# Attention block: merge of the two branches bank by bank, a gate input projected earlier, a key tile split earlier

## The chip, the cores and the metric

The kernel runs on one core of a Trainium2 chip. The metric is the device time in microseconds of one execution. Of the kernel before, three timed runs are given: 1705.27, 1705.39 and 1705.43 us, median 1705.39 us.

## The reference

Two transformer blocks over 256 tokens of width 1024 in float32. The change touches only the attention part of the second block:

```python
h = rms_norm_2(x, attn_norm_g)
q, k, v, f_logit, cb, cc, cu, ga, gb = split(h @ w_in)      # widths 512 x3, 8, 512 x3, 1024 x2
q, k = rms_norm_2(q per head, q_norm_g), rms_norm_2(k per head, k_norm_g)      # 8 heads of 64
log_f = log_sigmoid(f_logit + b_f)
y_att = forgetting_attention(q, k, v, log_f)      # causal softmax, logits plus the cumulated log_f
y_conv = cb * causal_short_conv(cc * cu, conv_w)
merged = sigmoid(ga) * (y_att @ w_out_att) + sigmoid(gb) * (y_conv @ w_out_conv)
x = x + merged @ w_o
```

Before it lie the first block (a mixer and a dense network, a mixer and eight experts), behind it a router with 16 experts in four groups and a last gated projection.

## The kernel before, in words

**Weights.** All weights come as tiles of 128 x 2048 float32 (1 MB). The SP queue loads them in one fixed order into a ring of six slots. Each tile is split in two float32r parts, so that a product is three matmuls (`three`, L1080: high x high, high x low, low x high): ACT copies the tile to `w_high` (`high(T)`, L671), then DVE makes `w_low` as the difference (`low(T)`, L1597). There are three places for split tiles, so `high(T)` waits until PE has used tile T-3. A slot of the ring is free, and SP loads tile T+6 into it, when `low(T)` is done. Every engine has its work in an order written out by hand; waits are semaphores (`used(eng, name)`: PE has used the tile).

**The tiles of this block**, counted from B: q 0, 1; k 2, 3; v 4, 5; cb 6, 7; cc 8, 9; cu 10, 11; four gate inputs of two tiles each 12 to 19; out_conv2 20, 21; out_att 22, 23; o 24 to 27. Tiles 28 and on belong to the expert stage behind.

**PE.** The eight PSUM banks hold 512 columns each. `project_T` (L1087) makes half of an input transposed in one bank, with 48 matmuls of 256 columns per tile. The order is: the eight columns of the forget gates, q (banks 0, 1), a small transpose for the gate logits, k (2, 3), v (4, 5), the cumulated gates in bank 7, mean squares of q in banks 6 and 7, the first cb tile, mean squares of k in banks 6 and 7, the second cb tile (4, 5), then cc (0, 1) after `qk_hat` 1 and cu (2, 3) after `qk_hat` 2 (L1470). Then eight gate tiles alternate in banks 4 and 5, with the attention's logits, transposes and value products between them. `out_chunks` (L1539) projects the two branches transposed, out_conv2 into banks 4 to 7 and out_att into banks 0 to 3, each with two tiles of 48 matmuls; a bank holds two of the eight chunks of model columns. Last `rows_of_model` (L1114) multiplies the merged rows with o, 24 matmuls of 512 columns per tile, into banks 4 to 7. In front of it stand six filler matmuls, `spare(4, 6)` (L1563).

**DVE and ACT at the start.** `move_logits` (L1842) copies the forget gates' sums out, does `low(B+2)` and waits for the transpose on PE. Then DVE and ACT hand the log-sigmoid to and fro (`log_step`), and only behind it stand `high(B+3)` (L923) on ACT and `low(B+3)` on DVE.

**q-hat and k-hat.** ACT takes the square root of the mean squares (`qk_std`), DVE a reciprocal of 1024 columns and a product (`qk_hat`): q-hat goes to `h`, which frees banks 0 and 1; k-hat goes to `uT`, which frees 2 and 3. `low(B+9)` stands between the two, `low(B+10)` behind the second.

**The merge.** DVE multiplies the sigmoid of gb with banks 4 to 7 (`conv_gated`). When half of out_att is whole (`rows_half`, two banks) `merge(0)` (L2184) multiplies the sigmoid of ga, 1024 columns, with two banks and adds the other branch; `merge(1)` does the rest; ACT copies each half to `hT_high` (L1003), and `merged_low` (L2189) makes the difference in `hT_low`. `low(B+25)` stands in front of `merge(0)`. PE waits for half m // 2 in front of tile m of o (L1565).

Of the kernel before, what the change touches and what calls it, by code (L numbers as in the profile page):

```python
# [16 lines left out]
KC = D // P  # L17
# [84 lines left out]
def build(nc, A, out):  # L102
    ctx = ExitStack()
    with ctx:
# [110 lines left out]
        def bank(b, n=1):  # L215
            return PS[:, b:b + n, :].rearrange("p b n -> p (b n)")
# [64 lines left out]
        ple_moved, logits_moved = sem("ple_moved"), sem("logits_moved")  # L281
        HALF_MIX, HALF_FFN, HALF_ATT, HALF_O, HALF_PLE, HALF_PG = (1, 5), 3, 7, 8, 10, 11
        BY_TILE = (1, 2, 3, 6)
# [20 lines left out]
        stored = sem("stored")  # L304


        def slot(s):
# [133 lines left out]
        def sparse_segment(e, s):  # L441
            assert s.base == len(names)
            stream.segment(e.made(s), e.trips)
            for i in range(e.trips):
# [11 lines left out]
        w2 = A["w_in_2"][0]  # L456
        two = [("q", 0), ("k", 512), ("v", 1024), ("cb", 1544), ("cc", 2056), ("cu", 2568),
               ("ga0", 3080), ("ga1", 3592), ("gb0", 4104), ("gb1", 4616)]
# [15 lines left out]
        def used(eng, name):  # L474

            eng.wait_ge(split_used, split_at[name] + 1)
# [170 lines left out]
        def _(act):  # L647
# [23 lines left out]
            def high(T):  # L671

                name = names[T]
                w = stream.arrived(act, name, 0 if name[0] in ("moe", "moe2") else None)
                if T >= SPLITS:
                    act.wait_ge(split_used, T - SPLITS + 1)
                act.activation(w_high[:, T % SPLITS, :], slot(w), ACT.Copy).then_inc(split_high, 1)  # L677
# [237 lines left out]
            B = BASE[4]  # L915
            high(B + 2)


# [3 lines left out]
            act.activation(hs[:, 4:6, :], hs[:, 2:4, :], ACT.Ln, bias=ones[:, 0:1]).then_inc(log_step, 1)  # L922
            high(B + 3)  # L923
            used(act, ("q", 1))
# [16 lines left out]
            act.activation(wk[0][:], bank(4, 2), ACT.Copy).then_inc(cbu_copied, 1)  # L941
            for T in range(10, 14):
                high(B + T)
            used(act, ("cu", 1))
            act.activation(wk[1][:], bank(2, 2), ACT.Copy).then_inc(cbu_copied, 1)
            high(B + 14)

# [54 lines left out]
            high(B + 25)  # L1002
            for k in range(2):  # L1003
                act.wait_ge(mT_sum, k + 1)
                act.activation(hT_high[:, 4 * k:4 * k + 4, :].rearrange("p c s -> p (c s)"), sgu[:, k, :],
                               ACT.Copy).then_inc(mT_high, 1)
# [22 lines left out]
        def _(pe):  # L1029
# [5 lines left out]
            def spare(b, n, part=router2_pair):  # L1035

                for k in range(n):
                    mm(PS[:, b, 0:320], flat_cols(part)[:, 0:P], flat_cols(part), start=True, stop=True)
# [430 lines left out]
            project_T(("cb", 1), 5)  # L1469
            for name, b, value in (("cc", 0, 1), ("cu", 2, 2)):  # L1470
                pe.wait_ge(qk_hat, value)
                for hf in range(2):
                    project_T((name, hf), b + hf)

# [44 lines left out]

            pe.wait_ge(qk_std, 2)  # L1520
            pe.wait_ge(cbu_copied, 1)
            gate(0, lambda step: logits(0, step // 2) if step % 2 else None)
            pe.wait_ge(cbu_copied, 2)
            pe.wait_ge(cc_used, 1)
# [14 lines left out]
            def out_chunks(name, b, half):  # L1539

                for m in range(2):
                    T = have((name, m))
                    wh, wl = split(w_high, T, 2), split(w_low, T, 2)
                    for c in range(KC):
                        a = slice(c * P, (c + 1) * P)
                        for k in range(2):
                            f = half + 2 * m + k
                            last = three(chunks(b, 4)[:, c, :], (wh[:, k, a], wl[:, k, a]),
                                         (yT_high[:, f, :], yT_low[:, f, :]),
                                         m == 0 and k == 0 and c % 2 == 0, m == 1 and k == 1, True)  # L1550
                        if name == "out_att" and m == 1 and c == 3:
                            last.then_inc(rows_half, 1)
                    last.then_inc(split_used, 1)

            pe.wait_ge(yconv_low, 1)
            pe.wait_ge(gates_act, 8)
            pe.wait_ge(att_yT, 1)
            out_chunks("out_conv2", 4, 4)
            pe.wait_ge(att_yT, 2)
            out_chunks("out_att", 0, 0)  # L1560
            pe.wait_ge(mT_sum, 1)
            pe.wait_ge(conv_gated, 2)
            spare(4, 6)  # L1563
            for m in range(4):
                pe.wait_ge(merged, 1 + m // 2)  # L1565
                rows_of_model(("o", m), h_rows, 4, m == 0, m == 3)
# [10 lines left out]
        def _(v):  # L1577
# [15 lines left out]
            def rest_of(out_, whole, part):  # L1593

                return tt(out_, whole, part.bitcast(F32), ALU.subtract)  # L1595
# [246 lines left out]
            def move_logits(b, n, k, between=None):  # L1842

                v.wait_ge(logits_ready, 2 * k - 1)
                copy(small_sums[0:2 * n, :], PS[0:2 * n, b, 0:S]).then_inc(logits_moved, 1)
                if between:
                    between()
                v.wait_ge(logits_ready, 2 * k)
# [217 lines left out]

            move_logits(6, HEADS, 2, lambda: low(B + 2))
            sums = PS[:, 7, 0:4 * HEADS].rearrange("p (t a e) -> p t a e", t=TT, a=2)
# [9 lines left out]
            stt(out=lf[:], in0=lf[:], scalar=0.0, in1=hs[:, 4:6, :], op0=ALU.min, op1=ALU.subtract).then_inc(log_step, 1)  # L2078
            for T in range(3, 8):
                low(B + T)  # L2080
# [8 lines left out]
            for o in range(2):  # L2089
# [3 lines left out]
            last.then_inc(qk_hat, 1)  # L2093
            low(B + 9)
            v.wait_ge(qk_std, 2)
            own.link(nc.vector.reciprocal(wk[3], wk[3]))
            stt(out=uT[:], in0=chunks(2), scalar=pcol[:, 37:38], in1=r[1], op0=ALU.mult,
                op1=ALU.mult).then_inc(qk_hat, 1)
            for T in range(10, 14):
                low(B + T)  # L2100

            v.wait_ge(cbu_copied, 2)
            cu = wk[1].rearrange("p (c s) -> p c s", c=CH)
# [77 lines left out]
            low(B + 24)  # L2181
            low(B + 25)

            def merge(k):  # L2184

                own.link(tt(sgu[:, k, :], sgu[:, k, :], bank(2 * k, 2), ALU.mult))
                tt(sgu[:, k, :], sgu[:, k, :], sgu[:, 2 + k, :], ALU.add).then_inc(mT_sum, 1)

            def merged_low(k):  # L2189

                v.wait_ge(mT_high, k + 1)
                rest_of(hT_low[:, 4 * k:4 * k + 4, :].rearrange("p c s -> p (c s)"), sgu[:, k, :],
                        hT_high[:, 4 * k:4 * k + 4, :].rearrange("p c s -> p (c s)")).then_inc(merged, 1)

            v.wait_ge(conv_gated, 2)
            v.wait_ge(rows_half, HALF_ATT)
            merge(0)
            used(v, ("out_att", 1))
            merge(1)
            merged_low(0)  # L2200
            merged_low(1)
            for T in range(26, 30):
                low(B + T)
# [31 lines left out]
```

## Time and profile before

| what | us |
|---|---|
| median of three timed runs | 1705.39 |
| the profiled execution | 1702.37 |
| its span, first to last instruction | 1700.6 |
| PE busy | 1629.0 |
| DVE busy | 1287.8 |
| ACT busy | 1015.0 |

The span and what lies around it (1.8 us) make the profiled execution's time. Times in the trace count from the first instruction. A matmul's record is longer than the distance at which the next one can start. Idle time is told with the instruction that ended it, under what released that; on an engine that is not late it costs nothing. The attention block lies between about 1262 and 1466 us.

### The profile page before, as it was taken

The page shows a single profiled execution, that of the slowest core. Times are in us where ns is not written, and L with a number is a line of the kernel's source. Part 1 is how long each engine was busy: PE and PEld are TensorE (multiplying, and loading weights), DVE is VectorE, ACT ScalarE, POOL GpSimd, SP SyncE. Part 2 cuts the span into 40 slices and gives each one's busy share as a digit, 9 for nine tenths or more (in the row PEclk, how much of TensorE's full clock was granted, in tenths as well). Part 3 has the DMA queues.
Part 4 walks back from the last instruction along what each step waited for, and adds up shares of the span by engine and source line. Part 5 has one row for each costly group of instructions (what it writes and reads, how often), then busy time and mean ns, then how long its engine had stood idle before and what let it go on. Part 6 is the DMA issues. An engine that isn't in the chain of part 4 may idle for free.

```text
span 1700.6 us, 23910 instructions
## 1 busy us (share of the span) xinstructions
PE 1629.0 (96%) x9497; PEld 1335.6 (79%) x9497; DVE 1287.8 (76%) x1147; ACT 1015.0 (60%) x882; POOL 21.7 (1%) x41
## 2 busy tenths in 40 slices
PE   6999999998899999999999999999979999899997
PEld 6979999897677776777767677777768898788886
DVE  5984444698688889888898888888855665568875
ACT  4654343466576767777676777766624453367753
POOL 2000000000000000000000000000000000000000
PEclk9999999999999999999999999999989999999999
DMA  9536656433598989999898998989854434469970
GB/s 285 199 112 199 197 175 197 136 125 119 207 372 311 369 304 369 344 343 377 307 373 301 373 369 316 374 307 385 297 186 149 149 124 149 136 213 309 306 260 26
DMA packets 240906, 431.54 MB, mean 254 GB/s; under 512 B 11556, under 2 KB 121664, under 8 KB 240832
## 3 DMA queue, kind: packets, MB, share of 16 engines
q1 hardware_dynamic: 239344, 426.17, 71.4%
q10 hardware_dynamic: 1488, 4.34, 0.7%
q8 instruction: 51, 0.84, 0.2%
q14 instruction: 23, 0.19, 0.0%
HBM read 429.44 MB, written 1.05 MB: 253 GB/s over the span
## 4 chain that ended last, share of the span: by engine, by line
PE 74%; issue 13%; DVE 9%; ACT 3%; DMA 1%; POOL 0%; DVEq 0%; ACTq 0%; SPq 0%; POOLq 0%
PE PS L1083 22%; PE PS L1085 22%; PE PS L1084 22%; DVE w_low L1595 3%; PE PS L1171 2%; PE PS L1300 2%; DVE x_res L1948 1%; PE PS L1353 1%; ACT w_high L677 1%; DVE h L1612 1%; ACT w_high L830 1%; DVE hT_low L1595 1%; DMA ring<-in_w_in_dram 1%; PE PS L1480 0%; ACT L830 0%
## 5 line engine op out<-in xcount | busy, mean ns | idle before, releaser
L1595 DVE TENSOR_TENSOR w_low<-ring,w_high 128x2048 fp32r<-128x2048 f32 x402 | 918.0, 2289 | 281.9 <-ACT w_high L677 147.6
L830 ACT ACTIVATE w_high<-ring 128x2048 fp32r<-128x2048 f32 x306 | 586.0, 1918 | 244.4 <-PE PS L1085 244.2
L1083 PE MATMUL PS<-w_high,hT_high 128*96 128x512 f32 (+3 forms) x1184 | 416.6, 352 | 9.9 <-DVE hT_low L1595 5.7
L1085 PE MATMUL PS<-w_high,hT_low 128*96 128x512 f32 (+3 forms) x1184 | 413.5, 349 | 0.0
L1084 PE MATMUL PS<-w_low,hT_high 128*96 128x512 f32 (+3 forms) x1184 | 411.9, 348 | 0.0
L677 ACT ACTIVATE w_high<-ring 128x2048 fp32r<-128x2048 f32 x96 | 182.9, 1911 | 134.9 <-PE PS L1085 131.1
L1083 PE MATMUL PS<-hT_high,w_high 128*128 128x256 f32 x832 | 241.4, 290 | 7.3 <-DVE hT_low L1595 4.5
L1083 PEld LDWEIGHTS PS<-w_high,hT_high 128*96 128x96 f32 (+1 forms) x1184 | 196.7, 166 | 58.7 <-DVE hT_low L1595 6.2
L1084 PE MATMUL PS<-hT_low,w_high 128*128 128x256 f32 x832 | 237.2, 285 | 0.0
L1085 PE MATMUL PS<-hT_high,w_low 128*128 128x256 f32 x832 | 237.1, 285 | 0.0
L1085 PEld LDWEIGHTS PS<-w_high,hT_low 128*96 128x96 f32 (+1 forms) x1184 | 196.7, 166 | 47.7
L1084 PEld LDWEIGHTS PS<-w_low,hT_high 128*96 128x96 f32 (+1 forms) x1184 | 196.8, 166 | 46.7
L1083 PE MATMUL PS<-w_high,yT_high 128*96 128x512 f32 (+1 forms) x568 | 227.3, 400 | 1.9 <-DVE yT_low L1595 1.7
L1085 PE MATMUL PS<-w_high,yT_low 128*96 128x512 f32 (+1 forms) x568 | 223.4, 393 | 0.0
L1084 PE MATMUL PS<-w_low,yT_high 128*96 128x512 f32 (+1 forms) x568 | 223.1, 393 | 0.0
L1083 PEld LDWEIGHTS PS<-hT_high,w_high 128*128 128x128 f32 x832 | 161.5, 194 | 12.9 <-DVE hT_low L1595 5.6
L1084 PEld LDWEIGHTS PS<-hT_low,w_high 128*128 128x128 f32 x832 | 161.4, 194 | 0.9 <-issue 0.5
L1085 PEld LDWEIGHTS PS<-hT_high,w_low 128*128 128x128 f32 x832 | 161.3, 194 | 0.0
L1083 PEld LDWEIGHTS PS<-w_high,yT_high 128*96 128x96 f32 (+1 forms) x568 | 96.0, 169 | 37.9 <-issue 2.4
L1085 PEld LDWEIGHTS PS<-w_high,yT_low 128*96 128x96 f32 (+1 forms) x568 | 95.9, 169 | 35.5
L1084 PEld LDWEIGHTS PS<-w_low,yT_high 128*96 128x96 f32 (+1 forms) x568 | 96.1, 169 | 33.5 <-issue 1.0
L1595 DVE TENSOR_TENSOR yT_low<-PS,yT_high 128x384 fp32r<-128x384 f32 (+3 forms) x70 | 45.1, 644 | 10.2 <-ACT yT_high L869 8.2
(302 smaller groups left out, 1239.5 us busy)
## 6 DMA issues: line engine op xcount, KB each, us to landing
ring<-in_moe_wg_dram SPq DMA_DIRECT2D x88, 1024.0 KB, 6.7
ring<-in_moe_wu_dram SPq DMA_DIRECT2D x88, 1024.0 KB, 7.3
ring<-in_moe_wd_dram SPq DMA_DIRECT2D x80, 1024.0 KB, 6.7
ring<-in_w_in_dram SPq DMA_DIRECT2D x36, 1024.0 KB, 6.2
ring<-in_w_gate_dram SPq DMA_DIRECT2D x16, 1024.0 KB, 6.6
ring<-in_w_up_dram SPq DMA_DIRECT2D x16, 1024.0 KB, 6.8
ring<-in_w_down_dram SPq DMA_DIRECT2D x16, 1024.0 KB, 5.4
ring<-in_ffn_wg_dram SPq DMA_DIRECT2D x11, 1024.0 KB, 5.4
```

The lines of the kernel that those rows point to most:

```text
L677: act.activation(w_high[:, T % SPLITS, :], slot(w), ACT.Copy).then_inc(split_high, 1)
L830: act.activation(w_high[:, (s.base + k) % SPLITS, :], slot(w), ACT.Copy).then_inc(s.high_taken, 1)
L1083: mm(o, left_high, right_high, start=first, stop=False, skip_group_check=shared)
L1084: mm(o, left_high, right_low, start=False, stop=False, skip_group_check=shared)
L1085: return mm(o, left_low, right_high, start=False, stop=last_one, skip_group_check=shared)
L1171: last = mm(chunks(1 if c == 3 else 3, 1)[:, 0, :], diag[:, 8 * (m % 2) + k - k0, :], cpad[:, c, k:k + S], start=(k == 0), stop=(k == (TAP ...
L1300: mm(PS[:, 2 * b, c * CAP:(c + 1) * CAP], h[:, t, (4 * b + c) * P:(4 * b + c + 1) * P], pick[:, t, :], start=(t == 0), stop=(t == TT - 1))
L1353: last = nc.tensor.transpose(PS[:, 6 + j % 2, c * CAP:(c + 1) * CAP], wk[2 + j % 2][0:CAP, c * P:(c + 1) * P], ident[0:CAP, 0:CAP])
L1595: return tt(out_, whole, part.bitcast(F32), ALU.subtract)
L1612: stt(out=dst[:, t, a], in0=x[:, t, a], scalar=rstd[:, t:t + 1], in1=(gain5 if n == 5 else gain)[:, a], op0=ALU.mult, op1=ALU.mult).then_i ...
L1948: tt(o, o, bank((6 + hf, 1 + 2 * hf)[t]), ALU.add).then_inc(s.added, 1)
```

## The change

- The stream of tiles has cu before cc, so cu is B+8, B+9 and cc B+10, B+11.
- `high(B+3)` moves in front of the forget gates' exponential on ACT, `low(B+3)` into `move_logits` behind `low(B+2)` on DVE.
- PE projects cu directly behind cb, into banks 6 and 7, after `qk_std` 2; then cc into banks 0 and 1, after `qk_hat` 1. The wait for `qk_hat` 2 goes to the first gate tile, with that for the copy of cu.
- DVE does `low(B+10)` ahead of the second reciprocal. ACT copies cu from banks 6 and 7, before `high(B+12)`.
- out_conv2's first tile does chunks 4 to 7 first, and waits for the last gate's sigmoid only before chunk 0.
- The merge goes by banks: `rows_half` is signalled after chunks 1, 3 and 5, and four quarters of 512 columns replace two halves on DVE and ACT. `low(B+25)` moves behind the low part of quarter 0. PE waits for quarter m before tile m of o. The fillers are gone. (`HALF_O` and the later counts grow by two.)

```diff
-        two = [("q", 0), ("k", 512), ("v", 1024), ("cb", 1544), ("cc", 2056), ("cu", 2568),
+        two = [("q", 0), ("k", 512), ("v", 1024), ("cb", 1544), ("cu", 2568), ("cc", 2056),
...
+        def quarter(k0, k):
+            return sgu[:, k0 + k // 2, (k % 2) * HALF:(k % 2 + 1) * HALF]
...
             high(B + 2)
+            high(B + 3)
             act.wait_ge(log_step, ABS_Z)
...
-            high(B + 3)
             used(act, ("q", 1))
...
             act.activation(wk[0][:], bank(4, 2), ACT.Copy).then_inc(cbu_copied, 1)
-            for T in range(10, 14):
+            high(B + 10)
+            high(B + 11)
+            used(act, ("cu", 1))
+            act.activation(wk[1][:], bank(6, 2), ACT.Copy).then_inc(cbu_copied, 1)
+            for T in range(12, 15):
                 high(B + T)
-            used(act, ("cu", 1))
-            act.activation(wk[1][:], bank(2, 2), ACT.Copy).then_inc(cbu_copied, 1)
-            high(B + 14)
...
-            for k in range(2):
+            for k in range(4):
                 act.wait_ge(mT_sum, k + 1)
-                act.activation(hT_high[:, 4 * k:4 * k + 4, :].rearrange("p c s -> p (c s)"), sgu[:, k, :],
+                act.activation(hT_high[:, 2 * k:2 * k + 2, :].rearrange("p c s -> p (c s)"), quarter(0, k),
                                ACT.Copy).then_inc(mT_high, 1)
...
-            for name, b, value in (("cc", 0, 1), ("cu", 2, 2)):
-                pe.wait_ge(qk_hat, value)
-                for hf in range(2):
-                    project_T((name, hf), b + hf)
+            pe.wait_ge(qk_std, 2)
+            for hf in range(2):
+                project_T(("cu", hf), 6 + hf)
+            pe.wait_ge(qk_hat, 1)
+            for hf in range(2):
+                project_T(("cc", hf), hf)
...
-            pe.wait_ge(qk_std, 2)
-            pe.wait_ge(cbu_copied, 1)
+            pe.wait_ge(qk_hat, 2)
+            pe.wait_ge(cbu_copied, 2)
             gate(0, lambda step: logits(0, step // 2) if step % 2 else None)
-            pe.wait_ge(cbu_copied, 2)
             pe.wait_ge(cc_used, 1)
...
-                    for c in range(KC):
+                    order = (4, 5, 6, 7, 0, 1, 2, 3) if name == "out_conv2" and m == 0 else range(KC)
+                    for c in order:
+                        if name == "out_conv2" and m == 0 and c == 0:
+                            pe.wait_ge(gates_act, 8)
...
-                        if name == "out_att" and m == 1 and c == 3:
+                        if name == "out_att" and m == 1 and c in (1, 3, 5):
                             last.then_inc(rows_half, 1)
...
-            pe.wait_ge(gates_act, 8)
+            pe.wait_ge(gates_act, 7)
...
-            pe.wait_ge(mT_sum, 1)
             pe.wait_ge(conv_gated, 2)
-            spare(4, 6)
             for m in range(4):
-                pe.wait_ge(merged, 1 + m // 2)
+                pe.wait_ge(merged, 1 + m)
...
-            move_logits(6, HEADS, 2, lambda: low(B + 2))
+            def first_lows():
+                low(B + 2)
+                low(B + 3)
+
+            move_logits(6, HEADS, 2, first_lows)
...
             low(B + 9)
+            low(B + 10)
             v.wait_ge(qk_std, 2)
             own.link(nc.vector.reciprocal(wk[3], wk[3]))
...
-            for T in range(10, 14):
+            for T in range(11, 14):
                 low(B + T)
+            used(v, ("cc", 1))
             v.wait_ge(cbu_copied, 2)
...
             def merge(k):
-                own.link(tt(sgu[:, k, :], sgu[:, k, :], bank(2 * k, 2), ALU.mult))
-                tt(sgu[:, k, :], sgu[:, k, :], sgu[:, 2 + k, :], ALU.add).then_inc(mT_sum, 1)
+                if k == 3:
+                    used(v, ("out_att", 1))
+                else:
+                    v.wait_ge(rows_half, HALF_ATT + k)
+                own.link(tt(quarter(0, k), quarter(0, k), bank(k), ALU.mult))
+                tt(quarter(0, k), quarter(0, k), quarter(2, k), ALU.add).then_inc(mT_sum, 1)
...
             v.wait_ge(conv_gated, 2)
-            v.wait_ge(rows_half, HALF_ATT)
             merge(0)
-            used(v, ("out_att", 1))
             merge(1)
             merged_low(0)
+            low(B + 25)
+            merge(2)
             merged_low(1)
+            merge(3)
+            merged_low(2)
+            merged_low(3)
```

## Rows read from the trace of the kernel before

**Rows 1.** The page, busy us, share of the span and instructions of each engine.
```profile
PE 1629.0 (96%) x9497; PEld 1335.6 (79%) x9497; DVE 1287.8 (76%) x1147; ACT 1015.0 (60%) x882; POOL 21.7 (1%) x41
```
**Rows 2.** Waits of PE from 1262 to 1468: total us, times, longest.
```profile
PE PS L1083 <- DVE hT_low L1595: 2.4, 1, 2.4
PE PS L1083 <- DVE w_low L1595: 1.6, 2, 0.9
...
PE PS L1038 <- DVE sgu L2187: 1.0, 1, 1.0
PE PS L1083 <- issue: 0.7, 1, 0.7
PE PS L1461 <- DVE negc L2083: 0.6, 1, 0.6
```
**Rows 3.** Timeline of PE (start, us, instruction, idle before): end of B+2.
```profile
1281.90 0.28 PE L1085 MATMUL PS<-hT_high,w_low 128*128 128x256 f32 x1
1283.11 0.39 PE L1083 MATMUL PS<-hT_high,w_high 128*128 128x256 f32 x1 [0.94 <-DVE w_low L1595]
```
**Rows 4.** Timeline of DVE: gate logits, w_low of B+3.
```profile
1276.26 0.17 DVE L2069 TENSOR_TENSOR lf<-PS,bf 128x16 f32<-128x16 f32 x1 [9.59 <-PE PS L1275]
...
1280.76 2.29 DVE L1595 TENSOR_TENSOR w_low<-ring,w_high 128x2048 fp32r<-128x2048 f32 x1 [1.26 <-ACT w_high L677]
```
**Rows 5.** Timeline of ACT: the forget gates' exponential.
```profile
1277.08 0.22 ACT L920 ACTIVATE hs<-hs 128x16 f32<-128x16 f32 x1 [13.83 <-DVE hs L2072]
```
**Rows 6.** Timeline of PE: the first matmul of the first q tile.
```profile
1263.82 0.42 PE L1083 MATMUL PS<-hT_high,w_high 128*128 128x256 f32 x1
```
**Rows 7.** Timeline of the SP queue: the block's first six loads.
```profile
1225.24 12.40 SPq L508 DMA_DIRECT2D ring<-in_w_in_dram  x6
```
**Rows 8.** Timeline of PE: the first matmul of cc, that of cu.
```profile
1318.95 0.39 PE L1083 MATMUL PS<-hT_high,w_high 128*128 128x256 f32 x1 [1.21 <-DVE h L2091]
...
1331.35 0.36 PE L1083 MATMUL PS<-hT_high,w_high 128*128 128x256 f32 x1 [0.62 <-DVE w_low L1595]
```
**Rows 9.** Timeline of DVE: w_low of B+9, second reciprocal, k-hat.
```profile
1318.93 2.29 DVE L1595 TENSOR_TENSOR w_low<-ring,w_high 128x2048 fp32r<-128x2048 f32 x1
1321.14 6.55 DVE L2096 RECIPROCAL work<-work 128x1024 f32<-128x1024 f32 x1
1327.72 1.28 DVE L2097 SCALAR_TENSOR_TENSOR uT<-PS,pcol,work 128x1024 f32<-128x1024 f32 x1
```
**Rows 10.** Timeline of ACT: second square root, w_high of B+10.
```profile
1312.04 1.12 ACT L938 ACTIVATE work<-PS,eps_c 128x1024 f32<-128x1024 f32 x1 [4.55 <-PE PS L1461]
...
1318.70 1.91 ACT L677 ACTIVATE w_high<-ring 128x2048 fp32r<-128x2048 f32 x1
```
**Rows 11.** Timeline of PE: the first matmul of out_conv2.
```profile
1415.18 0.36 PE L1083 MATMUL PS<-yT_high,w_high 128*128 128x256 f32 x1 [0.73 <-issue]
```
**Rows 12.** Timeline of PE: the fillers, the first matmul of o.
```profile
1439.46 1.15 PE L1038 MATMUL PS<-router_pair 128*128 128x320 f32 x6 [1.03 <-DVE sgu L2187]
1442.99 0.79 PE L1083 MATMUL PS<-w_high,hT_high 128*128 128x512 f32 x1 [2.38 <-DVE hT_low L1595]
```
**Rows 13.** Timeline of DVE: product of 512 columns, w_low of B+25, first merge product.
```profile
1383.22 0.69 DVE L2133 TENSOR_TENSOR work<-PS,rowsum 128x512 f32<-128x512 f32 x1
...
1434.73 2.29 DVE L1595 TENSOR_TENSOR w_low<-ring,w_high 128x2048 fp32r<-128x2048 f32 x1 [3.21 <-ACT w_high L677]
1436.94 1.21 DVE L2186 TENSOR_TENSOR sgu<-sgu,PS 128x1024 f32<-128x1024 f32 x1
```
**Rows 14.** Timeline of ACT: the sigmoid of the last gate tile.
```profile
1414.48 0.60 ACT L952 ACTIVATE sgu<-PS 128x512 f32<-128x512 f32 x1 [3.30 <-PE PS L1085]
```
**Rows 15.** Stretches: us, busy us of PE, PEld, DVE, ACT, POOL, PEclk, DMA, GB/s.
```profile
1443.00:1446.00 3.00, 3.00 (x7) 2.41 (x8) 2.43 (x2) 1.69 (x1) 0.00 (x0) 0.52 0.00 0
1446.00:1466.50 20.50, 20.50 (x92) 16.95 (x91) 9.02 (x5) 5.79 (x4) 0.00 (x0) 1.00 0.50 154
1480.00:1486.60 6.60, 6.18 (x27) 5.78 (x26) 4.74 (x30) 0.00 (x0) 0.00 (x0) 0.50 0.34 137
```

More of the change, by code:

```diff
@@ L281, in build @@
         ple_moved, logits_moved = sem("ple_moved"), sem("logits_moved")
-        HALF_MIX, HALF_FFN, HALF_ATT, HALF_O, HALF_PLE, HALF_PG = (1, 5), 3, 7, 8, 10, 11
+        HALF_MIX, HALF_FFN, HALF_ATT, HALF_O, HALF_PLE, HALF_PG = (1, 5), 3, 7, 10, 12, 13
         BY_TILE = (1, 2, 3, 6)
@@ L2078, in _ @@
             stt(out=lf[:], in0=lf[:], scalar=0.0, in1=hs[:, 4:6, :], op0=ALU.min, op1=ALU.subtract).then_inc(log_step, 1)
-            for T in range(3, 8):
+            for T in range(4, 8):
                 low(B + T)
@@ L2181, in _ @@
             low(B + 24)
-            low(B + 25)
             def merge(k):
-                own.link(tt(sgu[:, k, :], sgu[:, k, :], bank(2 * k, 2), ALU.mult))
-                tt(sgu[:, k, :], sgu[:, k, :], sgu[:, 2 + k, :], ALU.add).then_inc(mT_sum, 1)
+                if k == 3:
[4 more added lines that the diff above has]
+                tt(quarter(0, k), quarter(0, k), quarter(2, k), ALU.add).then_inc(mT_sum, 1)
             def merged_low(k):
                 v.wait_ge(mT_high, k + 1)
-                rest_of(hT_low[:, 4 * k:4 * k + 4, :].rearrange("p c s -> p (c s)"), sgu[:, k, :],
-                        hT_high[:, 4 * k:4 * k + 4, :].rearrange("p c s -> p (c s)")).then_inc(merged, 1)
+                rest_of(hT_low[:, 2 * k:2 * k + 2, :].rearrange("p c s -> p (c s)"), quarter(0, k),
+                        hT_high[:, 2 * k:2 * k + 2, :].rearrange("p c s -> p (c s)")).then_inc(merged, 1)
             v.wait_ge(conv_gated, 2)
-            v.wait_ge(rows_half, HALF_ATT)
             merge(0)
-            used(v, ("out_att", 1))
             merge(1)
             merged_low(0)
+            low(B + 25)
+            merge(2)
             merged_low(1)
+            merge(3)
+            merged_low(2)
+            merged_low(3)
             for T in range(26, 30):
```

## The prediction

> **What bounds the kernel now.** I read the page's table of busy time first [rows 1]: the reader is to see that TensorE (PE) is busy for 96% of the span. So VectorE (DVE), ScalarE (ACT) and the loads count only where PE stands still for them. The change touches only the attention block, about 1262 to 1466 us. There the view of waits [rows 2] shows how little PE stands still: seven waits, 7.5 us, of which the change aims at all but one of 0.6 us (the copy of the cumulated gates); the row of 1.2 us, left out there, comes with the second edit. For the last, the merge, the wait of 2.4 us is not the whole: six filler matmuls lie beside it and the clock falls behind it.
>
> To size each wait I use the idle time plus 0.16 us. In a run of matmuls with 256 columns one starts each 0.12 us though it lasts 0.28, so an idle stretch also loses the overlap. [rows 3] shows it: 1281.90 to 1283.11 is 1.21 us where 0.12 is usual, 1.09 lost; the idle time shown is 0.94.
>
> **Key tile split ahead of the forget gates: gain 1.1.** PE waits at 1283.11 for w_low of the second key tile (B+3). Why is it late? DVE stood idle for 9.59 us until 1276.26 for the gate logits and made this part only at 1280.76, after the gate arithmetic [rows 4]; ACT stood idle for 13.83 us until 1277.08 with the tile's `high` queued behind [rows 5]. In the new order `high(B+3)` may start when the first q tile is used. That tile starts at 1263.82 [rows 6]; six matmuls start 0.21 us apart while the clock is still low there, 42 at 0.12, which ends it at about 1270.1. ACT takes 1.9 us (1272.1), DVE 2.3 us (1274.4). Behind them wait the gates' first steps, which are released at 1276.2 by PE: 1.8 us of cover. Its landing is no risk: B+3 is one of the six loads issued between 1225.2 and 1237.6 [rows 7]. PE's wait goes; next late would be w_low of B+4, which ACT can start after its square at about 1279.9 and DVE ends near 1284.1, for a PE that wants it at 1288. Price 1.09 us, and 0 if `high` were held behind something else.
>
> **cu in front of cc: gain 2.15.** PE now waits 1.21 us for q-hat, which frees banks 0 and 1, and 0.62 us for w_low of tile B+10 [rows 8]. That is late because DVE does the second reciprocal (6.55 us) and u (1.28) ahead of it [rows 9]. In the new order PE goes from cb to cu, into banks 6 and 7, which the second square root has read by 1313.2 [rows 10], 4.5 us before PE comes at 1317.6. Its weights B+8 are there, and B+9 is made at 1318.93 to 1321.2 [rows 9], wanted at 1323.4. DVE then does `low(B+10)` first (high at 1318.70 to 1320.6 [rows 10]): 1321.2 to 1323.5, reciprocal to 1330.0, u to 1331.3, `low(B+11)` to 1333.6. PE wants B+10 at 1329.2, B+11 at 1335.0 and u only at the first logits, about 1341: cover 5.7, 1.4 and 9 us. ACT's copy of cu moves up (about 1329.5 to 1330.6), and the two `high` behind it are ready before PE. The product cc*cu waits for cc now, at 1341, and PE needs its end only a gate tile (12 us) later. The queue of SP loads the tiles in the new order, with the same sizes; each is issued by an older `low`. Gain 1.37 + 0.78 = 2.15; if B+11 were 2 us later it would take 0.6 back.
>
> **The last gate's wait moved: gain 0.9.** PE stands 0.73 us at 1415.18 [rows 11] for the sigmoid of gate 7, which the page calls issue because it has no releaser. The new code asks for gate 6 only, begins with banks 6 and 7, and asks for gate 7 after 24 matmuls (2.9 us), when it has long been read. 0.73 + 0.16 = 0.89.
>
> **Merge bank by bank: gain 4.7, and 1.4 of clock.** PE is idle for 1.03 us, runs the six fillers for 1.15, is idle for 2.38 and starts `o` at 1442.99 [rows 12]. With the 0.16 us of overlap 4.7 us are lost, the fillers included (they go). So out_att ends at 1438.4, and its last tile begins 48 matmuls of 0.12 us earlier, at 1432.5. With twelve matmuls a bank, banks 0 to 3 are whole at 1434.1, 1435.5, 1437.0 and 1438.4. DVE's sequence needs a price for 512 columns that this merge does not have. 1024 columns took 1.21 us a step, a product of 512 columns from PSUM 0.69 on DVE [rows 13], and 512 columns from PSUM 0.60 on ACT [rows 14]. The last two I take, since they have the width and the source of the new steps. Then (times of the old trace): product and sum of quarter 0 1434.15 to 1435.6; its high on ACT to 1436.2; quarter 1 on DVE to 1437.0; low of quarter 0 to 1437.6. PE wants it at 1438.3: 0.7 us to spare. `low(B+25)`, at 1434.73 before [rows 13], moves behind it: 1437.6 to 1439.9, wanted at 1443.8. Quarter 2 to 1441.3, low 1 to 1441.9 (wanted 1443.8), quarter 3 to 1443.3, low 2 to 1443.9, low 3 to 1444.6 (wanted 1449.3 and 1454.8). What is queued behind the new waits: on ACT `high(B+26)` behind the fourth quarter, 1444.0 to 1445.9, and on DVE its low to 1448.2, wanted at 1449.3, 1.1 us to spare. The load that `low(B+25)` frees is issued 2.8 us later, for a tile that is read near 1490. So all 4.7 us go.
>
> From 1443.0 to 1446.0 the granted clock is 0.52, near 1.2 of 2.4 GHz, and seven matmuls take 3.0 us; from 1446 on 92 take 20.5 [rows 15], 0.22 each, so seven would take 1.6. PE had stood still but for the fillers; without that pause the fall has no cause: 1.4 us more.
>
> Against a split speaks the Trainium skill ("Advanced Engine Details and Errata", The Read-Write Bubble): each instruction of DVE and ACT exposes a fixed latency, so tiles should be large. The rows agree: two halves of 0.69 us cost 0.17 more than one of 1.21. By that rule the six DVE steps that are halved cost 1.0 us more, all of it inside the slack above, and the sum stays.
>
> **Sum.** 1.1 + 2.15 + 0.9 + 4.7 + 1.4 = 10.2 us. Everything behind starts when `o` ends and PE has the same waits there in the same order, so it carries over. The profiled execution took 1702.37 us (span 1700.6, 1.8 around it), so 1692.1. It is 3.0 below the median of the timed runs, 1705.39; I take the same difference and forecast **1695.1**. The clock part is the least certain. Its bounds: none of it (8.8, 1696.5), since a fall may lie elsewhere in the timed runs; and the later stretch at 0.50, 1480 to 1486.6 [rows 15], might also go. PE is the late one there for about 5.1 us and would do that work in half, 2.6 more: 12.8, 1692.5. The skill ("TensorE: Matmul & The Clock Gate", The HAM clock gate) says that the number of slow matmuls at a ramp varies between runs of one kernel; no run here shows that yet.
>
> **Rivals.**
> A: the merge becomes a new wait. If a 512-column step cost as much as one of 1024 (1.24 us, with 0.03 for the hand-over from step to step), quarter 0 would be ready at 1440.2 and `o` start 1.8 late, its second tile 0.5 later for `low 1`, its third 2.2 late, because w_low of B+26 stands behind the fourth quarter: 4.5 back, gain 5.7, 1699.7. At worst the merge gains nothing: 4.1, 1701.3. For it speaks that slacks are 0.7 and 1.1 us; against it are the two 512-column rows [rows 13, 14]. Chance 0.10.
> B: the clock gives it back, the case that ends slower. Place: the router and the first group of the second expert stage, where it was at 0.50 for 6.6 us already and the short waits of PE now come at other moments. Each us at 0.50 costs half a us if PE is late, so 20.5 us more of it eat the whole gain and 27 us give 1708.8. The one stretch that I read there is a third as long. Same within 0.2% 0.03 (13.6 to 27 us more), slower 0.03.
> C: the forecast with its bounds, 1692.5 to 1696.5: 0.84.
>
> **How the numbers follow.** 0.2% (3.4 us) is about what a measurement here can tell from no change. C and A lie beyond it: faster 0.94. B gives 0.03 and 0.03. The range goes from the low bound of C to the first time of A: 1692.5 to 1699.7.
>
> **What would show it.** Right: no idle time of PE in front of the second k tile, the first cu tile, the first cc tile, out_conv and `o`; the last out_att matmul and the first `o` matmul 0.12 to 0.3 us apart; clock 1.00 there; `o` ends some 10 us earlier. Wrong: PE waits for hT_low or w_low inside `o` (A), a wait in front of the first logits for u, or a longer stretch at 0.50 after the router (B).

## The result

| what | before | after |
|---|---|---|
| median of the timed runs, us | 1705.41 (4 runs, 1705.27 to 1705.82) | 1692.47 (4 runs, 1691.48 to 1693.74) |
| profiled execution, us | 1702.37 | 1693.24 |
| its span, us | 1700.6 | 1691.4 |
| block: first q tile to last o matmul, us | 202.6 | 191.9 |

The ratio is 0.9923 with a 95% interval of 0.991 to 0.9935: 12.9 us faster, where 10.3 were forecast. The median lies just below the low end of the range (1692.5).

The page of after, its part on busy time, which answers to [rows 1]:

```profile
PE 1625.9 (96%) x9491; PEld 1334.8 (79%) x9491; DVE 1288.5 (76%) x1153; ACT 1015.6 (60%) x884; POOL 21.7 (1%) x41
```

DVE has six instructions and 0.7 us more, ACT two and 0.6 us: the halved steps. PE has the six fillers less.

The waits of PE in after, from 1262 to 1458 (total us, times, longest), which answer to [rows 2]:

```profile
PE PS L1270 <- DVE hT_low L1601: 3.3, 1, 3.3
PE PS L1465 <- DVE negc L2093: 0.6, 1, 0.6
```

The first ends in front of the block's first q tile. Inside the block only the wait of 0.6 us is left that the change did not aim at. The reader is to see that six waits went and none came. In the timeline of PE the first matmul of out_conv2 and that of o follow their predecessors (the answers to [rows 11] and [rows 12]):

```profile
1411.83 0.28 PE L1089 MATMUL PS<-hT_high,w_low 128*128 128x256 f32 x1
1411.95 0.28 PE L1087 MATMUL PS<-yT_high,w_high 128*128 128x256 f32 x1
...
1434.87 0.28 PE L1089 MATMUL PS<-yT_high,w_low 128*128 128x256 f32 x1
1434.99 0.40 PE L1087 MATMUL PS<-w_high,hT_high 128*128 128x512 f32 x1
```

0.12 us lie between the starts in both places. The timeline of DVE in after shows the merge:

```profile
1430.94 0.69 DVE L2201 TENSOR_TENSOR sgu<-sgu,PS 128x512 f32<-128x512 f32 x1 [2.72 <-PE PS L1089]
1431.66 0.69 DVE L2202 TENSOR_TENSOR sgu<-sgu 128x512 f32<-128x512 f32 x1
1432.31 0.69 DVE L2201 TENSOR_TENSOR sgu<-sgu,PS 128x512 f32<-128x512 f32 x1
1433.03 0.69 DVE L2202 TENSOR_TENSOR sgu<-sgu 128x512 f32<-128x512 f32 x1
1433.64 0.69 DVE L1601 TENSOR_TENSOR hT_low<-sgu,hT_high 128x512 fp32r<-128x512 f32 x1
1434.24 2.28 DVE L1601 TENSOR_TENSOR w_low<-ring,w_high 128x2048 fp32r<-128x2048 f32 x1
```

Each step of 512 columns takes the 0.69 us of [rows 13]. hT_low of quarter 0 is ready at 1434.33, 0.66 us before PE starts o. The low part of B+25 comes behind it.

The clock, in stretches of after (us, busy us of PE, PEld, DVE, ACT, POOL, PEclk, DMA share, GB/s; answers to [rows 15]): the end of out_att with all of o, and the router.

```profile
1435.00:1457.00 22.00, 22.00 (x100) 18.23 (x99) 16.21 (x13) 8.71 (x7) 0.00 (x0) 1.00 0.59 191
1470.00:1478.00 8.00, 7.30 (x34) 6.89 (x34) 5.24 (x32) 0.24 (x1) 0.00 (x0) 0.57 0.33 131
```

The fall of the clock behind the merge is gone, the one behind the router is still there.

So the block gained 10.7 us in the two traces, close to the sum of 10.2. The timed runs gained 2.2 more. Where is the rest, and is it the change's? Two theories went into the runs. **T**, the clock: the timed runs of before pay more for stretches at the lower clock than its first trace shows. **R**, the block: the timed executions of before have waits that the trace does not show.

### The profile page after: what moved, and what is told of

Its sections match the earlier page's. It is cut to its first block, busy times and chain, and to the rows that moved or that the text cites. A ratio compares the mean times of both kernels' runs of the same rounds, so it can differ in the third digit from the quotient of the medians.

```text
span 1691.4 us, 23906 instructions
## 1 busy us (share of the span) xinstructions
PE 1625.9 (96%) x9491; PEld 1334.8 (79%) x9491; DVE 1288.5 (76%) x1153; ACT 1015.6 (60%) x884; POOL 21.7 (1%) x41
## 4 chain that ended last, share of the span: by engine, by line
PE 84%; DVE 8%; ACT 4%; issue 3%; DMA 1%; POOL 0%; DVEq 0%; ACTq 0%; SPq 0%
PE PS L1087 25%; PE PS L1089 25%; PE PS L1088 25%; DVE w_low L1601 3%; PE PS L1175 2%; PE PS L1304 2%; ACT w_high L833 1%; DVE x_res L1954 1%; PE PS L1357 1%; DVE hT_low L1601 1%; DVE h L1618 1%; PE PS L1042 1%; ACT w_high L680 1%; DMA ring<-in_w_in_dram 1%; ACT yT_high L872 1%
## 5 line engine op out<-in xcount | busy, mean ns | idle before, releaser
L1087 PEld LDWEIGHTS PS<-w_high,hT_high 128*96 128x96 f32 (+1 forms) x1184 | 195.9, 165 | 53.7 <-DVE w_low L1601 5.0
L1601 DVE TENSOR_TENSOR yT_low<-PS,yT_high 128x384 fp32r<-128x384 f32 (+3 forms) x70 | 45.1, 644 | 10.2 <-ACT yT_high L872 8.2
```

Of the source, the lines that this page charges most:

```text
L1087: mm(o, left_high, right_high, start=first, stop=False, skip_group_check=shared)
```

## Four traces of before, two of after

The kernels before and after, unchanged, once more:

> The kernel before once more, for its trace beside timed runs of the same chip. The timed runs were 3.0 us longer than the profiled execution of the trace that the sum used. Theory T (the clock): the block from the first q tile to the last o matmul takes 202.6 us in every execution, as in the old trace (1263.8 to 1466.4), and the 3 us lie in stretches at the lower clock elsewhere, so that an execution of 1705.4 shows one or two more stretches with a granted clock of 0.50 outside the block than one of 1702.4. Rival R (the block): an execution of 1705.4 has a longer block, near 205 us, by waits that the old trace does not show. Timed ratio to itself 1.000.

> The changed kernel once more. Its runs so far lie at 1691.5 to 1693.7. T: its block takes 191.9 us in every execution, and runs of 1691.6 and 1693.5 differ by one stretch of 1.7 us at the lower clock outside of it. R: the block itself varies by 2 us. Both: about 12.5 to 13 us below the kernel before, timed.

> A third trace of the kernel before. So far: first q tile at 1263.8 and 1265.0, block 202.6 and 204.0 us, rest of the span 234.2 and 235.3 us, at 1702.4 and 1706.2 us. Theory T: the block is 202.6 or 204.0 us, as one stretch at 0.50 behind the merge is short (about 3.4 us) or long (about 6.8 us), with nothing else in it that differs. Rival R2: the length behind the merge is always the longer one and the old trace is the exception for another reason.

> A fourth trace, as the third: block 202.6 or 204.0 us by T, start of the first q tile between 1263.5 and 1266.6 and rest of the span between 233.5 and 235.5 us, whichever kernel it is.

Each trace is cut at the first matmul of the first q tile and at the end of the last one of o. All in us; the last two columns are stretches at a granted clock of 0.50 (1.2 GHz). "Router" is the part from the end of o to the first expert tile.

| trace | whole | up to q | block | behind | low clock behind the merge | low clock in the router |
|---|---|---|---|---|---|---|
| before, first | 1702.4 | 1263.8 | 202.6 | 234.2 | one, 3.4 | one, 6.8 |
| before_third | 1702.8 | 1264.2 | 202.6 | 234.2 | one, 3.4 | one, 6.8 |
| before_again | 1706.2 | 1265.0 | 204.0 | 235.3 | one, 6.8 | two, 6.8 each |
| before_fourth | 1707.3 | 1266.1 | 204.1 | 235.5 | one, 6.8 | two, 6.8 each |
| after, first | 1693.2 | 1265.0 | 191.9 | 234.4 | none | one, 6.8 |
| after_again | 1692.3 | 1265.3 | 191.5 | 233.7 | none | one, 6.8 |

At half the clock PE loses at most half of such a stretch, and less where the stretch also covers a pause. The product with o, from its first to its last matmul, takes 23.4 us in the first two rows, 24.9 in the next two and 22.0 in both of after: the low clock costs it 1.4 or 2.9 us in before and nothing in after. I call the first two rows short executions and the next two long ones.

The 49 timed runs of before that were taken beside the experiments lie between 1702.46 and 1707.20 us with no gap over 0.6, so the two kinds are what four traces show, not all that occurs. Their mean granted clock is 0.986 on average (0.984 to 0.988), that of the short traces 0.987, of the long ones 0.986; the eight timed runs of after have 0.988 or 0.989. Beside after_again 17 runs of before have a median of 1705.57. after_again lies at 1692.34 to 1693.57 (4 runs), ratio 0.9932 with an interval of 0.9915 to 0.9948. The stretches of before_again from behind the merge through the router, in the same columns as those of after above:

```profile
1444.00:1451.00 7.00, 6.97 (x18) 5.49 (x19) 3.48 (x2) 1.74 (x1) 0.00 (x0) 0.56 0.22 59
1451.00:1469.00 18.00, 18.00 (x82) 14.89 (x81) 8.01 (x4) 5.75 (x3) 0.00 (x0) 1.00 0.48 153
1474.00:1481.00 7.00, 5.60 (x24) 4.07 (x24) 5.73 (x8) 4.86 (x6) 0.00 (x0) 0.51 0.23 75
1481.00:1484.00 3.00, 1.46 (x8) 1.08 (x8) 2.38 (x11) 0.24 (x1) 0.00 (x0) 1.00 0.50 150
1484.00:1492.00 8.00, 7.33 (x36) 7.33 (x37) 4.02 (x28) 0.00 (x0) 0.00 (x0) 0.57 0.18 75
```

The reader is to see 18 matmuls of o in 7 us where 82 take 18: at the pace of the latter 18 take 3.95, so the fall behind the merge costs 3.05 us here (2.9 by the length of the whole product), against 1.4 in the first trace. The pause in front of it is the same to 0.01 us in all four. In the timeline of PE of before_again:

```profile
1440.50 1.15 PE L1038 MATMUL PS<-router_pair 128*128 128x320 f32 x6 [1.03 <-DVE sgu L2187]
1444.03 0.79 PE L1083 MATMUL PS<-w_high,hT_high 128*128 128x512 f32 x1 [2.38 <-DVE hT_low L1595]
```

So R falls for the traced executions: the waits in the block do not differ, the clock behind them does. T in the form that the expectation for before_again gives it missed too: it put the whole difference outside the block, and 1.4 of the 3.8 us lie in it, with 1.2 up to q and 1.1 behind. What holds is the clock as the cause, at more than one place. The block of after, 191.9 in every execution by T, was 191.5 in the second; R's 2 us did not show. Rival R2 of the third trace (the old trace an exception) falls, and before_fourth came within its forecast bounds.

The router does not divide the kernels as the merge does. The second low stretch is in no trace of after, but two kernels further on that differ from after only at the merge (after_6_fillers, after_dve_late) have one of 10.2 us there and need 26.6 and 26.5 us from o to the first expert tile, as long as the long executions of before (26.4 and 26.5); the short ones need 25.3, after 25.4 and 25.2. So this us comes and goes in both families.

## One part at a time

**The merge alone.** Edit: the hunks of the merge, nothing else.

```diff
-                        if name == "out_att" and m == 1 and c == 3:
+                        if name == "out_att" and m == 1 and c in (1, 3, 5):
...
-            spare(4, 6)
             for m in range(4):
-                pe.wait_ge(merged, 1 + m // 2)
+                pe.wait_ge(merged, 1 + m)
...
-            low(B + 25)
...
             merge(0)
...
             merge(1)
             merged_low(0)
+            low(B + 25)
+            merge(2)
+            merged_low(1)
+            merge(3)
+            merged_low(2)
+            merged_low(3)
```

> The kernel before with only the merge by banks (and without the fillers). By the steps of the sum the block gains 4.7 us of standing still and 1.4 us of clock, 6.1 together: from the first q tile to the last o matmul 196.5 us. T: timed gain between 4.5 and 8, since low-clock stretches elsewhere may move. Were the merge a new wait (rival A of the prediction) the block would gain 1.5 or less.

Block 195.9 us, 6.7 less than in the short executions of before and 8.1 less than in the long ones. No low clock lies behind the merge, but two stretches of 6.8 us lie in the router, with no pause of the merge in front of them. Timed 1698.04 us (5 runs), ratio 0.996 (0.9946 to 0.9974): 7.5 us. The waits of PE in it (from 1262 to 1461) are those of [rows 2] without the two of the merge:

```profile
PE PS L1086 <- DVE w_low L1596: 1.6, 2, 0.9
PE PS L1086 <- DVE h L2092: 1.2, 1, 1.2
PE PS L1086 <- issue: 0.7, 1, 0.7
PE PS L1464 <- DVE negc L2084: 0.6, 1, 0.6
```

**Everything but the merge.** Edit: the changed kernel with the merge of before, its order of lows and its fillers.

```diff
+            spare(4, 6)
             for m in range(4):
-                pe.wait_ge(merged, 1 + m)
+                pe.wait_ge(merged, 1 + m // 2)
...
```

> The changed kernel with the old merge and its fillers. By the sum 1.1 + 2.15 + 0.9 = 4.1 us less than before: block 198.3 us or a little less. If the parts add, this gain and that of merge_only make 10.6 in the block; the timed gains need not add if the clock elsewhere falls differently (T), and must add to about 12.9 by R.

Block 198.45 us, 4.1 less than 202.6, with a short stretch (3.4 us) behind the merge. Timed 1699.96 us (7 runs), ratio 0.997 (0.9959 to 0.9982): 5.6 us. The two timed gains make 13.1 us, the whole change 12.9 and 12.4; each interval is 4 to 5 us wide, so the parts add as well as it can be told. R asked for that sum and T left it open, so this pair of runs does not speak for T; the traces do. The key tile's split and the gate's wait have no run of their own: for them stand the waits that are gone and the length of the block here.

**cu in front of cc alone.** Edit, in extract (ACT copies cu in the place that it has in the whole change):

```diff
-        two = [("q", 0), ("k", 512), ("v", 1024), ("cb", 1544), ("cc", 2056), ("cu", 2568),
+        two = [("q", 0), ("k", 512), ("v", 1024), ("cb", 1544), ("cu", 2568), ("cc", 2056),
...
-            for name, b, value in (("cc", 0, 1), ("cu", 2, 2)):
-                pe.wait_ge(qk_hat, value)
-                for hf in range(2):
-                    project_T((name, hf), b + hf)
+            pe.wait_ge(qk_std, 2)
+            for hf in range(2):
+                project_T(("cu", hf), 6 + hf)
+            pe.wait_ge(qk_hat, 1)
+            for hf in range(2):
+                project_T(("cc", hf), hf)
...
             low(B + 9)
+            low(B + 10)
             v.wait_ge(qk_std, 2)
...
```

> The kernel before with only cu in front of cc. The prediction's term is 2.15 us. From the transpose of the gate logits to the first transpose of the attention's output (both before the merge, so that its clock is not in it) the kernel before takes 132.2 us; 130.0 us here, with no idle time in front of the first cu and the first cc matmul. If DVE's later reciprocal held PE up at the first logits, less than 1 us would be gained.

From the transpose of the gate logits to the last transpose of the attention's output it takes 129.85 us (1278.17 to 1408.02) where before takes 132.16 (1275.93 to 1408.09): 2.3 us for the term of 2.15. (The expectation says first transpose; the 132.2 us in it are those to the last.) No idle time is left in front of the first cu and the first cc matmul. The waits of PE in it, from 1262 to 1436, are the key tile's, the last gate's and the one that the change does not aim at, behind the 3.3 us that end in front of the block:

```profile
PE PS L1084 <- DVE w_low L1597: 0.9, 1, 0.9
PE PS L1084 <- issue: 0.7, 1, 0.7
PE PS L1462 <- DVE negc L2085: 0.6, 1, 0.6
```

## The clock term and the cover, each by itself

**Twelve more fillers in before.** Edit:

```diff
-            spare(4, 6)
+            spare(4, 18)
```

> The kernel before with 18 filler matmuls in front of o where it has 6. They end at about 1442.9, when the hT_low that PE waits for is ready, so that o starts no later, and PE stands still for 1 us there where it stood for 3.4. This takes the clock term alone out of the merge. T (the clock, of which the timed runs pay more than the old trace): no stretch at 0.50 behind the merge; block 201.1 us, 1.5 less than in the old trace and 2.9 less than in the newer one (203.96), and a timed gain of 1.5 to 3. R (the merge's gain lies in its waits only): the timed gain is 0 to 0.5.

In the timeline of PE:

```profile
1441.31 2.90 PE L1038 MATMUL PS<-router_pair 128*128 128x320 f32 x18 [1.03 <-DVE sgu L2187]
1444.83 0.50 PE L1083 MATMUL PS<-w_high,hT_high 128*128 128x512 f32 x1 [0.62 <-DVE hT_low L1595]
```

and in the stretches, the end of out_att and all of o at the full clock:

```profile
1438.00:1467.00 29.00, 27.35 (x136) 23.11 (x135) 18.22 (x12) 9.73 (x7) 0.00 (x0) 1.00 0.47 147
```

The pause has its old length (the first o matmul starts 3.5 us behind the first filler in both kernels), but PE is at work in it (1.65 us of idle time are left, where 1 was expected), and the clock stays. The block is 201.18 us, 1.4 less than the short and 2.8 to 2.9 less than the long executions; since o starts no earlier behind the fillers, that is the clock term alone. Timed 1702.88 us (10 runs) against 1704.72 (13 runs), ratio 0.9988 (0.9978 to 0.9998): 1.8 us, between the 1.4 that the sum took and the 3.05 of before_again. The interval (0.3 to 3.8 us) does not tell more, and the timed gain need not be the merge's alone: this trace has two low stretches in the router as well, of 3.4 and 6.8 us.

**DVE late in front of quarter 0.** Edit in the changed kernel:

```diff
+                if k == 0:
+                    for _ in range(2):
+                        own.link(tt(wk[4][:, 0:HALF], wk[4][:, 0:HALF], wk[4][:, HALF:D], ALU.mult))
                 own.link(tt(quarter(0, k), quarter(0, k), bank(k), ALU.mult))
```

> The changed kernel with two more DVE products of 512 columns (0.69 us each) in front of the first quarter's product; they compute nothing that is used. The prediction gave quarter 0 a cover of 0.7 us: the first o matmul should start 0.7 us later than behind an uninterrupted out_att, with an idle time of about 0.7 us ended by hT_low. If the cover is zero, 1.4 us; if it is above 1.4 us, nothing.

The timeline of PE, end of out_att and start of o:

```profile
1436.20 0.28 PE L1089 MATMUL PS<-yT_high,w_low 128*128 128x256 f32 x1
1437.17 0.47 PE L1087 MATMUL PS<-w_high,hT_high 128*128 128x512 f32 x1 [0.69 <-issue]
```

and that of DVE, the two products and hT_low of quarter 0:

```profile
1432.27 1.42 DVE L2203 TENSOR_TENSOR work<-work 128x512 f32<-128x512 f32 x2 [2.72 <-PE PS L1089]
1436.38 0.68 DVE L1601 TENSOR_TENSOR hT_low<-sgu,hT_high 128x512 fp32r<-128x512 f32 x1
```

The view calls the wait issue; hT_low is ready at 1437.06, 0.11 us before the first o matmul, so I take it for the releaser. The two products take 1.42 us, and o starts 0.97 - 0.12 = 0.85 us late: the cover is 0.6 us, not zero and not above 1.4. The block is 192.6 us, 0.9 longer than the mean of the two traces of after (191.7), so no second wait comes of it. Rival A was 0.6 us away: beyond that, what DVE loses PE should lose too, which one delay of this size does not measure.

**Six fillers kept.** Edit in the changed kernel:

```diff
             pe.wait_ge(conv_gated, 2)
+            spare(4, 6)
             for m in range(4):
```

> The changed kernel with the six fillers kept in front of o. At the full clock six take 0.13 us each, so the block is 0.8 us longer (192.5 instead of 191.7) and the timed run 0.8 us longer: the fillers cost their own time as soon as the wait behind them is gone. If they still held up the clock for what follows, the timed run would not be longer.

Block 192.64 us, 0.9 longer than 191.7. Timed 1693.67 us (4 runs, 1692.03 to 1694.87), ratio 0.9936 (0.9919 to 0.9952), against 1693.15 and 0.9932 of after_again: the 0.8 us can't be told from nothing in these timed runs, but the block shows it. The fillers cost their own time and bring nothing once the wait is gone.

## A version that gains more

In after PE waits 1.94 us in front of the router's transpose, because DVE makes w_low of B+30 ahead of the copy of the logits. Edit of the first version:

```diff
-            low(B + 30)
             later = route2()
-            sweeps(moe2, main2, rest2, restream2, 2, later)
+            def tables_then_low():
+                later()
+                low(B + 30)
+            sweeps(moe2, main2, rest2, restream2, 2, tables_then_low)
```

> The changed kernel with low(B+30) moved from in front of the router to behind its tables. In the trace of after DVE makes this part from 1466.05 to 1468.3 while PE waits 1.94 us for the logits' copy behind it. The copy can start 1.4 us earlier, so PE loses 1.4 us less there; the part is wanted near 1494. Timed 1.4 us less than the changed kernel, and 2 to 3 less if the stretch at 0.50 behind the router goes as well.

The first matmul behind that wait, in after and in this kernel:

```profile
1468.73 0.31 PE L1279 MATMUL PS<-ident,work 40*128 40x40 f32 x2 [1.94 <-DVE work L1851]
...
1468.48 0.31 PE L1279 MATMUL PS<-ident,work 40*128 40x40 f32 x2 [0.51 <-DVE work L1851]
```

The wait is 0.5 us instead of 1.94. Not all of it reaches the end: from o to the first expert tile PE needs 24.5 us where after needs 25.4 and 25.2, so 0.7 to 0.9 of the 1.4 us arrive there, and the whole part behind o is 233.6 us against 234.4 and 233.7. Timed 1691.7 us (4 runs, 1691.24 to 1693.57), ratio 0.9921 (0.9904 to 0.9937): by the ratios 1.9 us better than after_again (0.9932) and 0.3 better than after's first runs (0.9923). The intervals overlap, so a shorter wait is shown, and a gain in the whole time is not. The low stretch in the router stayed:

```profile
1471.00:1479.00 8.00, 7.26 (x34) 7.26 (x35) 6.28 (x29) 0.00 (x0) 0.00 (x0) 0.57 0.00 0
```

The second version adds fillers where PE still stands:

```diff
                 small_turned(2, ne, 2 * k - 1)
+                if k == 2:
+                    spare(4, 6)
                 pe.wait_ge(exps_wanted, k)
-                spare(4, (14, 6)[k - 1])
+                spare(4, (14, 11)[k - 1])
```

> The changed kernel with low(B+30) moved behind the router's tables and 11 more fillers in the router: 6 in front of the logits' maximum and 11 instead of 6 in front of the mask. The router's stretch at 0.50 costs PE 3.1 to 3.3 us in the traces of after. If PE standing still is its cause, it goes and the timed run is 3 us below the changed kernel with only the low moved; if the fillers run at the lower clock all the same, they are in the way and it is 0.5 to 1 us slower than that kernel.

```profile
1456.00:1482.00 26.00, 20.86 (x158) 18.61 (x158) 16.60 (x55) 11.45 (x17) 1.10 (x2) 1.00 0.30 102
```

The clock is at its full level (2.4 GHz) from the end of o to the first expert tile. PE gets there in 21.8 us instead of 24.5: 2.7 of the 3 us expected, in this trace. Timed 1690.8 us (5 runs, 1688.49 to 1690.90), ratio 0.9913 (0.9899 to 0.9926): the fastest kernel here, 14.9 us below before, and by the ratios 1.7 and 3.2 us below the two measurements of the changed one, with intervals that overlap. Against the kernel with only the low moved the ratios make it 1.4 us, half of what was expected; one of the five runs, the traced one, is 3 us below that kernel. The other four lie about 2 us above the traced run, though their mean granted clock is 0.989 to 0.991 and that of the traced run 0.989, so the mean clock does not account for them. Why they are slower is open.

## Why the prediction missed its range

Point by point, by its own steps:

- **Key tile, 1.1; gate wait, 0.9.** Right: the waits are gone. DVE made the key tile's w_low from 1273.45 to 1275.7, 1.7 us before the gate logits, cover 1.8 by the working. From the gate logits' transpose to the first matmul of the cumulated gates after takes 23.37 us, before 24.56: 1.2 for 1.1.
- **cu and cc, 2.15.** Right, 2.3 in swap_only.
- **Merge, 4.7 by prices of 0.69 and 0.60 us.** Right: both waits and the fillers went (from the last transpose of the attention's output to the first o matmul 34.6 us before, 28.9 after, 5.7 for 4.7 and 0.9 together). The DVE steps took 0.69, the ACT copies 0.63 from SBUF; the cover of quarter 0 was 0.66 where 0.7 was worked out, and 0.6 in after_dve_late. The Trainium skill's rule of a fixed cost per instruction ("Advanced Engine Details and Errata", The Read-Write Bubble) holds in the sum, 0.7 us more DVE work, and does not decide, because DVE was not late.
- **The block's sum.** 10.2 forecast, 10.7 measured against the first trace.
- **The clock term, 1.4.** Mis-sized. It came from one trace, a short execution: 1.4 there and in before_third, 3.05 in before_again and as much in before_fourth (both 24.9 us for o where after takes 22.0); 1.8 timed by before_18_fillers.
- **"I take the same difference"**, the 3.0 us between the profiled execution and the timed median. This step failed. I treated the 3.0 us as a constant that both kernels have; for after it is -0.8, so 3.8 us came that the forecast did not have. 0.4 more came from the block (10.69 for the sum's 10.25), and 1.6 went the other way, since after's profiled execution took 1.2 us more up to q than before's first and 0.2 more behind o: 2.6 in all. The long executions show where such a difference can lie. Against the first trace they are 1.2 and 2.3 us longer up to q, 1.4 and 1.5 in the block behind the merge, 1.1 and 1.3 in the router. Only the middle part is bound to the kernel before: after has no pause there and no fall of the clock. How often a timed execution of before pays it can't be counted, as only four are traced; so of the 2.2 us that the timed runs gained beyond the block's 10.7, up to 1.5 are shown to be the change's, and the rest is not traced to a place.
- **The lower bound, 1692.5.** It let the router's stretch disappear (2.6 us), which did not happen, and had nothing for a before that pays more than its trace (2.6 us by the sum above). The measured 1692.47 lies 0.03 us below it because these two errors all but cancel. That is luck.
- **Rival B**, a clock that gives the gain back in the router, did not come: behind o the two traces of after take 234.4 and 233.7 us, the four of before 234.2 to 235.5. Rival A did not come.

What stays open: what decides the length of the fall behind the same pause, and the second stretch in the router. With the pause unchanged (1.03 and 2.38 us around the fillers) the fall began 0.5 to 0.7 us before o's first matmul in the four traces of before, 0.5 us behind it in all_but_merge and 1.5 us behind it in swap_only, where it was short and cost o 1.7 us. Two low stretches in the router are also in merge_only, swap_only and before_18_fillers. These executions differ in when they reach the place, and no run set this time alone. The Trainium skill ("TensorE: Matmul & The Clock Gate", The HAM clock gate) says that the number of slow matmuls at a ramp varies between runs of one kernel; the four traces of before agree, with 1.4 us lost behind one and the same pause in two and 2.9 in two.

## What to carry to other kernels

A wait that is split into quarters costs a little more work on the helper engine and frees the late one, as long as the first quarter is ready in time: work out that cover, since from there on the path is the helper's. Where PE pauses, count the clock behind the pause as well, and from more than one execution: here it was about a third of what the merge's waits were in two traces and about two thirds in two others. Before a difference between a profiled execution and the timed runs is carried over to a changed kernel, find out which stretch it lies in.

## What was not expected of the hardware

- The same pause of PE (1.03 us, six fillers of 1.15 us, 2.38 us, equal to 0.01 us in four traces) was followed by 3.4 us at 1.2 GHz in two executions and by 6.8 us in two others.
- The time up to the first q tile, which the change does not touch, varied from 1263.7 to 1266.6 us over the fourteen traced executions. The five with a stretch at 1.2 GHz of 10.2 us near 430 us lie at 1265.7 to 1266.6, the nine with 3.4 us there at 1263.7 to 1265.3.
- PE working at 18 fillers kept the full clock through a pause in the real work of 3.5 us (before_18_fillers, one trace), and o started as long behind the first filler as with six.
